# Expert gates of a PEER layer: a table of gates written by indirect DMAs of single elements, in place of one-hot products on TensorE

## The reference, cut to what matters

```python
q = (hf @ wq).reshape(T, PEER_HEADS, 2, PEER_HALF)
s = jnp.einsum('thcd,hcnd->thcn', q, subkeys).astype(jnp.float32)
sv, si = lax.top_k(s, PEER_TOPK)
cand = sv[:, :, 0, :, None] + sv[:, :, 1, None, :]
cidx = si[:, :, 0, :, None] * PEER_NKEYS + si[:, :, 1, None, :]
fv, fpos = lax.top_k(cand.reshape(T, PEER_HEADS, PEER_TOPK * PEER_TOPK), PEER_TOPK)
fidx = jnp.take_along_axis(cidx.reshape(...), fpos, axis=-1)
gates = jax.nn.softmax(fv, axis=-1).astype(h.dtype)
...
    act = jax.nn.gelu(jnp.einsum('chkd,cd->chk', u, xc), approximate=False)
    return jnp.einsum('chk,chkd->cd', gc * act, vv)
```

## Time and profile before

| | us |
|---|---|
| median of 3 runs | 2102.42 (2101.3 to 2102.5) |
| the profiled execution, its time | 2104.01 |
| the profiled execution, its span | 2102.3 |
| PE busy | 1918.7 |
| DVE busy | 1428.1 |
| ACT busy | 734.1 |
| POOL busy | 550.0 |

### The profile page before, as it was taken

The page is one execution under the profiler, slowest core; times in us unless marked ns, Lnnn a source line. Parts: engine busy times, 40 slices in busy tenths (PEclk is TensorE's granted clock), DMA queues, the critical chain, the costliest instruction groups (busy, mean ns, idle before and its releaser), DMA issues.

```text
span 2102.3 us, 33108 instructions
## 1 busy us (share of the span) xinstructions
PE 1918.7 (91%) x10322; PEld 1602.1 (76%) x10322; DVE 1428.1 (68%) x2902; ACT 734.1 (35%) x1305; POOL 550.0 (26%) x427
## 2 busy tenths in 40 slices
PE   2889896786967999999999999999989999999996
PEld 2343585685834687879999999999988888888885
DVE  4187435445244468687488888886758888888887
ACT  1221134343222343435444444443233333333331
POOL 3011332131100222223432233224513323233310
PEclk9999998998989999999999999999999999999998
DMA  7273100000051232434589889889979999999982
GB/s 262 98 233 127 41 1 1 0 0 0 0 201 42 90 126 96 132 99 133 206 294 299 298 296 301 296 301 336 389 281 414 368 347 359 355 353 348 355 316 79
DMA packets 244203, 434.82 MB, mean 207 GB/s; under 512 B 84578, under 2 KB 157636, under 8 KB 244164
## 3 DMA queue, kind: packets, MB, share of 16 engines
q1 hardware_dynamic: 207300, 300.12, 41.2%
q0 software_dynamic: 36864, 134.23, 17.5%
HBM read 379.77 MB, written 54.53 MB: 207 GB/s over the span
## 4 chain that ended last, share of the span: by engine, by line
PE 65%; DVE 1%; DMA 1%; issue 1%; ACT 0%; SPq 0%; ACTq 0%; DVEq 0%
PE bank L1315 25%; PE bank L1706 8%; PE bank L1704 8%; PE bank L1705 8%; PE bank L1641 5%; PE bank L1295 5%; PE bank L1687 4%; DMA urows<-in_peer_u 1%; PE bank L1653 1%; DVE n_stats L1118 0%; DVE wide L2008 0%; DVE wide L2006 0%; DVE wide L1127 0%; SPq L1539 0%; SPq L1543 0%
## 5 line engine op out<-in xcount | busy, mean ns | idle before, releaser
L1315 PE MATMUL bank<-hh,uh 128*128 128x384 f32 x1024 | 358.3, 350 | 0.0
L1315 PE MATMUL bank<-hl,uh 128*128 128x384 f32 x1024 | 344.4, 336 | 0.0
L1704 PE MATMUL bank<-vh,wh 128*128 128x512 f32 x768 | 299.4, 390 | 3.1 <-DVE wl L1967 3.1
L1706 PE MATMUL bank<-vh,wl 128*128 128x512 f32 x768 | 299.5, 390 | 0.0
L1705 PE MATMUL bank<-vl,wh 128*128 128x512 f32 x768 | 299.4, 390 | 0.0
L1373 POOL DMA_INDIRECT vsel<-in_peer_v,picks x128 | 151.7, 1185 | 413.0 <-DVE gt L1399 398.7
L1800 ACT ACTIVATE vh<-vraw 128x1024 fp32r<-128x1024 f32 x128 | 135.9, 1062 | 288.4 <-PE bank L1706 270.2
L1373 POOL DMA_INDIRECT usel<-in_peer_u,picks x108 | 147.9, 1369 | 247.9 <-DVE usel L1380 234.6
L1964 DVE TENSOR_TENSOR vl<-vraw,vh 128x1024 fp32r<-128x1024 f32 x128 | 156.6, 1223 | 81.1 <-ACT vh L1800 81.0
L1315 PE MATMUL bank<-hh,ul 128*128 128x384 f32 x1024 | 198.3, 334 | 0.0
L1315 PEld LDWEIGHTS bank<-hl,uh 128*128 128x128 f32 x1024 | 194.4, 190 | 0.0
(11 more groups left out here) (314 smaller groups left out, 3096.3 us busy)
## 6 DMA issues: line engine op xcount, KB each, us to landing
urows<-in_peer_u SPq DMA_DIRECT2D x128, 512.0 KB
vraw<-in_peer_v SPq DMA_DIRECT2D x128, 512.0 KB
ada<-in_ada_w SPq DMA_DIRECT2D x12, 2048.0 KB
scored<-act_out SPq DMA_DIRECT2D x128, 192.0 KB
gates<-SS SPq DMA_DIRECT2D x16, 1536.0 KB
gtile<-gates SPq DMA_DIRECT2D x32, 768.0 KB
act_in<-scored SPq DMA_DIRECT2D x128, 192.0 KB
wt<-in_w_in SPq DMA_DIRECT2D x19, 512.0 KB
```

What stands on the lines that cost most here:

```text
L1315: last = pe.matmul(bank, u[:, k, :], h[:, k, :], start=(n == 0), stop=(n == 3 * KD - 1))
L1704: pe.matmul(b, wh[s][:, cols], vh[s][:, half], start=first, stop=False)
L1706: last = pe.matmul(b, wl[s][:, cols], vh[s][:, half], start=False, stop=stop)
```

## The change

The dense table of gates is filled another way.

- **Clearing.** `gates` is now `[128, 128, 384]`, one plane for each second half of an expert's number. It is filled with zeros during mixing: SP issues 16 DMAs of 1.5 MB from a zero column of `vtok` and waits for them at the stage's end.
- **Routing.** Every head's softmax is made in the routing loop: the subtraction of the maximum as DVE writes `FV`, the exponential on ACT two turns later (`exponential`), sum, reciprocal and two products on DVE (`share`). DVE also works out `places`, the address in the table of each of a token's 16 gates.
- **Putting.** POOL adds the gates into the table with `put_gates`: one indirect DMA with `compute_op=ALU.add` for each head, pick and token tile, each of 128 elements of 4 bytes to 128 addresses. These are 8 x 16 x 3 = 384 DMAs. They stand between POOL's other work: 6 after every remainder in turns 3 to 7, 2 after every remainder in turns 8 and 9, 12 after the fetches of each turn 10 to 25, 20, 20 and 16 after those of turns 26 to 28. The first DMA of a head waits until all of the head before have landed.
- **Gone:** `hot_step` on DVE, its 384 products on PE, 96 copies on ACT, the 16 stores of 1.5 MB by SP, and the softmax and the nine transposes between turns 9 and 10.
- The V stage reads its gates in pieces of 1536 bytes instead of 6144; SP waits for all `put` semaphores before it loads the first.

```diff
+            for j in range(16):
+                sp.dma_start(flat[:, 24 * j:24 * j + 24, :], vtok[:, 0:1, :].broadcast_to([P, 24, P]))\
+                    .then_inc(cleared, 16)
+            sp.wait_ge(cleared, START + 16 * 16)
...
-            with pool.Fori(0, SPREAD) as i:
+            def put_gates(n):
+                for h, k, t in islice(places_of, n):
+                    if k == 0 and t == 0:
+                        pool.wait_ge(picks_up, START + 2 * h + 2)
+                        pool.wait_ge(gate_up, START + 2 * h + 5)
+                        if h:
+                            pool.wait_ge(put[h - 1], 16 * (NT - 1) * TOPK)
+                    at = (h * TOPK + k) * (NT - 1) + t
+                    pool.indirect_dma_start(out=grid, out_offset=bass.IndirectOffsetOnAxis(
+                        ap=places[:, at:at + 1], axis=0), in_=FV[:, t, h + 2, k:k + 1], in_offset=None,
+                        compute_op=ALU.add).then_inc(put[h], 16)
+            for i in range(SPREAD):
                 for s in range(4):
                     scores.remainder(pool, i, s)
+                    if i >= 3:
+                        put_gates(6 if i < ROUTED else 2)
...
-            pool.wait_ge(picks_up, START + 1)
-            for i in range(BLOCKS):
+            pool.wait_ge(picks_up, START + 2 * HEADS)
+            for i in range(TURNS):
                 fetched(0, 3, 3 * i, 3)
+                put_gates(12)
             pool.wait_ge(scores.ul_up, START + 4 * SPREAD + 1)
             for i in range(LAST - CLEAR):
                 fetched(0, 4, LATER + 4 * i, 3 if i == 0 else 4)
+                put_gates(20)
...
-                    for j, q in enumerate(steps_of(s)):
-                        if len(steps_of(s)) == 2:
-                            scores.product(pe, i, s, True, j)
-                        else:
-                            scores.product(pe, i, s, True)
-                        n = STEPS * (i - SPREAD) + q
-                        pe.wait_ge(hot, START + n + 1)
-
-                        pe.wait_ge(staged, START + n - 2)
-                        for k in range(4):
-                            last = pe.matmul(banks[4 + q % SLOTS][:, k * P:(k + 1) * P], OI[q % SLOTS][:, k, :],
-                                             OJ[q % SLOTS][:, k, :], start=True, stop=True)
-                        last.then_inc(spread, 1)
...
+                    share(step, h)
...
-                    dve.tensor_copy(FV[:, :, bass.ds(h, 1), :].rearrange("p t o k -> p t (o k)"), fv[:, :, :])
+                    dve.tensor_tensor(FV[:, :, bass.ds(h + 2, 1), :].rearrange("p t o k -> p t (o k)"), fv[:, :, :],
+                                      fv[:, :, 0:1].broadcast_to([P, NT, TOPK]), ALU.subtract).then_inc(less_up, 1)
```

More of the change, by code:

```diff
@@ L3 @@
 from contextlib import ExitStack
+from itertools import islice
 import math
@@ L23 @@
 TD = T - P
-BLOCKS = 16
-TB = TD // BLOCKS
-STEPS = TB // 4
+TURNS = 16
 ROUTED = 8
@@ L1297, in turn, with product @@
             last.then_inc(self.turned, 1)
-    def product(self, pe, i, s, late, part=None):
+    def product(self, pe, i, s, late):
         bank, uh, ul = self.banks[s % 2][:, 0:TD], self.uh[s % 2], self.ul[s % 2]
-        if part in (None, 0):
-            pe.wait_ge(self.uh_up, START + 8 * i + 2 * s + 2)
-            pe.wait_ge(self.gelu_up, START + 4 * i + (s - 1))
+        pe.wait_ge(self.uh_up, START + 8 * i + 2 * s + 2)
+        pe.wait_ge(self.gelu_up, START + 4 * i + (s - 1))
         steps = [x for k in range(KD) for x in ((uh, k, self.hh), (uh, k, self.hl))]
         steps += [(ul, k, self.hh) for k in range(KD)]
-        for n in range(3 * KD) if part is None else range(12 * part, 12 * part + 12):
+        for n in range(3 * KD):
             if n == 2 * KD:
@@ L1409, in emit_pick @@
     for work, dst in ((cand, IS), (cand2, JS)):
-        last = dve.tensor_reduce(dst[:, :, bass.ds(h, 1), :].rearrange("p t o k -> p t (o k)"),
-                                 work[:, :, :, :], AX.X, ALU.add)
+        last = dve.tensor_reduce(dst[:, :, :], work[:, :, :, :], AX.X, ALU.add)
     step(last)
@@ L1457, in emit_experts @@
         act_in = sb("act_in", [P, 4, TD])
-        gt = [sb(f"gtile{q}", [P, BLOCKS, 4, TB]) for q in range(2)]
+        gt = [sb(f"gtile{q}", [P, 4, TD]) for q in range(2)]
         w = [sb(f"w{b}", [P, TD]) for b in range(2)]
@@ L1463, in emit_experts @@
         x1s = urows
[L1464 to L1472, removed]
+        lg, lb = (m[:, :, :].rearrange("p s t -> p (s t)")[:, 0:D] for m in (gt[0], act_out))
         scores = ExpertScores(sem, banks, ident, hh, hl, peer_u, urows, uraw, uh, ul, act_out, scored)
@@ L1480, in emit_experts @@
         iota_up, picked, p_dve, p_soft = (sem(n) for n in ("iota_up", "picked", "p_dve4", "p_soft"))
[L1481 to L1484, removed]
+        less_up, exp_up, gate_up = (sem(n) for n in ("less_up", "exp_up4", "gate_up4"))
+        put = [v["bare"](f"put{h}") for h in range(HEADS)]
         v_in = [sem(f"v_in{s}") for s in range(4)]
@@ L1555, in _ @@
                 sp.wait_ge(sk_in[c], START + 16 * HEADS)
-                sp.wait_ge(sent[c], START + 16 * (BLOCKS // 2))
+            for h in range(HEADS):
+                sp.wait_ge(put[h], 16 * (NT - 1) * TOPK)
             load_gates(0, 0)
@@ L1825, in _, with share @@
         def _(dve):
-            per = 14
+            per = 17
             chain = Tally(p_dve)
-            dve.wait_ge(iota_up, START + 1)
+            for k in range(2):
+                dve.memset(FV[:, :, k, :], 0.0).then_inc(less_up, 1)
+            dve.wait_ge(iota_up, START + 2)
+            def share(step, h):
+                top = FV[:, :, bass.ds(h, 1), :].rearrange("p t o k -> p t (o k)")
+                dve.wait_ge(exp_up, START + h + 1)
+                dve.wait_ge(gate_up, START + 2 * h)
+                step(dve.tensor_reduce(tot[:, :], top, AX.X, ALU.add))
+                step(dve.reciprocal(tot[:, :], tot[:, :]))
+                dve.tensor_tensor(top[:, 0:NT - 1], top[:, 0:NT - 1],
+                                  tot[:, 0:NT - 1].unsqueeze(2).broadcast_to([P, NT - 1, TOPK]), ALU.mult)\
+                    .then_inc(gate_up, 1)
+                dve.tensor_tensor(shares[:, bass.ds(TOPK * h, TOPK)], top[:, NT - 1],
+                                  tot[:, NT - 1:NT].broadcast_to([P, TOPK]), ALU.mult).then_inc(gate_up, 1)
             with dve.Fori(0, HEADS // 2) as g:
```

168 lines of the change are left out of this document (62 added, 106 removed).

## The result

| | before | after |
|---|---|---|
| median of 4 runs, us | 2101.86 (2099.1 to 2102.5) | 2411.95 (2407.88 to 2418.0) |
| span of the profiled execution, us | 2102.3 | 2410.5 |
| granted clock of PE, mean of the span | 0.964 | 0.897 |

The changed kernel takes 1.148 times as long, 95% interval 1.145 to 1.151: 310 us more where 95 were forecast. The page of after: the span, the engines' busy time, PE and POOL in 40 slices, the granted clock, POOL's DMA queue, the chain by engine and by line, and the group of the puts.

A forecast was written before the change was run, and what follows sets the result against it. PE bounds the kernel before; with the change POOL was to be the bound. 2104.0 + 32 (turns 3 to 7) + 2 (8 and 9) + 61 (10 to 28) = 2199, median 2197 us; range 2060 to 2430.

The forecast's parts named there:

- the price of a put: On POOL: a put costs what a fetch does, 0.94 + 0.30 = 1.24 us undisturbed, 1.33 to 1.42 with hindrance.
- turns 10 to 28, with (a) and (b): POOL's 368 fetches and puts at 1.42 us plus 15 of head waits, 538 us against 477: +61.
- (a): Turns 10 to 25: six one-hot steps of 0.89 us of PE go from each turn, -85 us if PE stays the bound.
- (b): Between turns 9 and 10: PE's 5.8 us softmax wait and 2.9 us of slow work after it go, -8.7 us.
- POOL the bound from turn 3: POOL busy nearly throughout turns 3 to 7 and 10 to 28; turns of 42 us in routing, 26 in spreading.
- The hindrance by DVE: DVE products with two SBUF sources delay POOL's DMAs: a put takes 1.33 us in routing, 1.42 in turns 10 to 28.
- The waits between heads: Turns 10 to 28: five waits of 3 us, 15 together; a rival had 15 us each, 2270 us, sharing 0.13.
- Zeros, DVE, ACT, loads of gates at nothing: Work added outside POOL, from mixing to the V stage, is hidden: 0 us; uncovered, the zeros would cost 126.
- A put is cheaper than a fetch: Rival on POOL: at 0.97 us with gap PE is the bound again, some 2010 to 2030 us; chance 0.19.
- A put is dearer: Rival on POOL: adding needs the old element too, 2.2 us a put, 2505 us; chance 0.13, shared with head waits.
- The DMA engines as the bound: Rival: at 171 ns a packet puts fill the DMA engines, 36.5 us a turn in 10 to 25, 2424 us; chance 0.11.
- the low end, all at 1.24: All puts and fetches undisturbed: +21 + 0 - 16 = +5, 2107 us.

The follow-up runs named there:

- e2_plain: The changed kernel with every put as a plain indirect write, without the adding; 2197.11 us.
- e1_noput: The changed kernel without the 384 puts and without the waits for them; 2012.12 us.
- e8_early: The kernel before with only the head-by-head softmax in routing and the transposes between turns 8 and 9; one-hots stay, no puts; 2102.39 us, ratio 0.9998.
- e4_half: The changed kernel with adding puts for partitions 0 to 63 only, 64 elements each; 2350.95 us.
- e10_early_fetch: e8_early with the transposes behind the second product of turn 9 and turn 10's six fetches between turn 9's remainders; 2094.74 us, ratio 0.9968.

## Why the prediction was wrong in size

**The step that failed** is the price of a put: "I take the same price for a put", 1.24 us undisturbed, because a put has as many addresses as a fetch. Addresses were not what differed. Measured undisturbed: 1.54 + 0.30 = 1.84 us, 0.60 more, of which plain writes show 0.01 to 0.02 (e2_plain). The upper bound in the prediction, 2 x 0.94 + 0.30 = 2.2 for adding, named the right cause, the adding; I gave it too little weight, for want of a row. Why the adding takes POOL longer no run shows. An operation with a flag that no row of the trace has was priced by its kin without that flag.

The terms, with the 1.24 replaced and the formula kept. In after's routing 120 puts took 198.68 us, 1.66 each; from 1135 to 1650, 191 puts and 311.09 us, 1.63.

| term | forecast | formula at the measured price | measured |
|---|---|---|---|
| turns 3 to 7 | +32 | 5 x (10.4 + 24 x 1.96 - 36.0) = +107 | +106 |
| turns 8 and 9 | +2 | 2 x (10.4 + 8 x 1.93) - 40.4 = +11 | +7.5 |
| turns 10 to 28, with (a) and (b) | +61 | 248 x 1.93 + 170 + 15 - 477 = +187 | +194 |
| V stage | 0 | 0 | 0 |
| sum | +95 | +305 | +308 |

One price gives 210 of the 213 us that were missing. It is taken from after's own trace; that the adding is what makes it is shown by e2_plain. The measured +194 is what lies between turn 9's end and the first product of the V stage, 1862.10 - 1127.57 = 734.5 us after and 1553.84 - 1013.65 = 540.2 before.

**Point by point.**
- *(a) and (b), -85 and -8.7.* Right in sum: by the traces e1_noput gained 91.9 of 93.7. The missing 2 us lie at (b), where the landing of the first fetch is late next (1.7 us of PE), and the prediction had named nothing. That the 8.7 come only if nothing else is waited for is shown by e8_early, which had (b) alone and gained nothing, since the transposes then waited for the last head.
- *POOL the bound from turn 3.* Right, by its waits in turns 3 to 7 and by the chain from turn 10 on. The turns are longer than forecast, by the price: 57 us for 42 in routing (285.8 / 5), 32 for 26 in spreading.
- *The hindrance by DVE.* Right in size. At plain price the puts of e2_plain took 116.13 / 112 = 1.04 us in routing and 297.64 / 273 = 1.09 later, 0.08 and 0.14 over the undisturbed 0.95; forecast 0.09 and 0.18. By the Trainium skill ("SBUF — State Buffer", Who interferes with whom) only DVE work that uses the port pair shared with GpSimd holds it up; the trace agrees, since the 1.3 us that all of routing's DVE work would have made of a plain put were not seen.
- *The waits between heads.* Forecast five of 3 us from turn 10 on; measured 7 of 18.0 us together, of which two small ones (1.36 and 0.91 us) are in turns 5 and 7, and five of 3.1 us later. The rival of 15 us each is out: a put lands in 3.3 us, 6.9 at most.
- *Zeros, DVE, ACT, loads of gates at nothing.* Right within 2 us, by e1_noput.
- *A put is cheaper than a fetch.* Out: for 128 elements never under 0.94 us, even for 4 bytes and without the adding. It would have needed 1.14 with its gap.
- *A put is dearer.* This is what happened, at 1.84 undisturbed in place of 2.2, and so at 2412 in place of 2505.
- *The DMA engines as the bound.* It named 2424, close to the result, for the wrong reason. The DMA share is 0.69 from 1135 to 1650, and of the chain there only the 3.2% of the waits between heads is DMA. Puts of half the elements (80 packets for 144, e4_half) take only 61 us off, of which 384 x 0.145 = 56 are POOL's own time. A time that fits is no evidence for a mechanism.
- *A slip in the range.* By its own formula the low end, all at 1.24, is 368 x 1.24 + 15 - 477 = -6 for turns 10 to 28 and not -16, so 2117 and not 2107. The five products with two sources in routing are 17% of a turn and not 15%, which adds 0.01 us to a put. Neither changes the outcome.

## What to carry to other kernels

Count what each small DMA costs the engine that issues it, gap included, before moving work off TensorE: 384 puts of 1.93 us are 741 us of POOL to save 85 us of PE. Where the new instruction carries a flag that the trace has no row for, the range should be weighted as unknown, and a kernel with only that instruction in place of its nearest kin is the first thing to run. A good idea that overloads one engine can still pay in part: with a third of the puts, sized to POOL's spare time, and the first fetches of the next stage moved up, this kernel gains 1.4% where the full change loses 14.8%. Of the 1.4%, 0.3% come without any put (e10_early_fetch), most of them from the transposes, which no longer wait for the last head.

## What was not expected of the hardware

- An indirect write that adds takes POOL 1.54 us, a plain one 0.95. Between 64 and 128 elements the first grows by 2.3 ns an element and the second by 1.0. The Trainium skill ("DMA: Bandwidth & Descriptors", SWDGE vs HWDGE vs iDMA) lets only GpSimd issue a DMA that accumulates, so no other engine could take the work; no run here tried one, and the page has no price for it.
- Adding makes a packet for each element: 144 a put of 128 elements and 80 a put of 64, so 16 and one for each. A plain put makes 32 for either size.
- For POOL, reading 4 bytes for each of 128 partitions (0.947 us) is no cheaper than fetching 4 KB for each (0.94).
- In the one run of plain puts of 64 elements ACT waited up to 47.7 us for a releaser taken to be a store of another queue; in the other runs it waited 8.2 us at most for such a releaser, and not at all in after. The cause is open.
